# A two-layer block kernel on one Trainium2 core: the first slab after two norms runs on x before the norm's root is known

## The reference

```python
# end of layer 0
hx = hx + g2 * swiglu(fx, ffn_w1[0], ffn_w3[0], ffn_w2[0])
# layer 1: convolution mixer, then feed-forward
ax = modulate(rms_norm(hx, norm_mix[1]), sh1, sc1)      # x*rstd*gain*(1+scale) + shift
yx = conv_mixer(ax, conv_w_in[0], conv_w[0], conv_w_out[0])
hx = hx + g1 * yx
fx = modulate(rms_norm(hx, norm_ffn[1]), sh2, sc2)
hx = hx + g2 * swiglu(fx, ffn_w1[1], ffn_w3[1], ffn_w2[1])   # (silu(f @ w1) * (f @ w3)) @ w2
```

## Time and profile before

| | |
|---|---|
| time, median of 3 runs | 2349.04 us (2348.41 to 2349.38) |
| the profiled execution's own time | 2346.38 us |
| its span in the profile | 2344.7 us |
| TensorE busy | 2243.8 us, 96% |
| VectorE busy | 1129.1 us, 48% |
| ScalarE busy | 729.9 us, 31% |
| GpSimd busy | 29.4 us, 1% |
| mean granted TensorE clock | 0.979 |

### The profile page before, as it was taken

How to read it: one execution, slowest core, us unless ns; L and a number is a source line. 1 busy time by engine, 2 the same in 40 slices (tenths; PEclk the granted TensorE clock), 3 DMA queues, 4 the chain that set the end, 5 groups by cost and what they waited for, 6 DMA issues and landing times.

```text
span 2344.7 us, 25372 instructions
## 1 busy us (share of the span) xinstructions
PE 2243.8 (96%) x9752; PEld 1748.0 (75%) x9752; DVE 1129.1 (48%) x1420; ACT 729.9 (31%) x951; POOL 29.4 (1%) x60
## 2 busy tenths in 40 slices
PE   6999999999899999989989999999999988999996
PEld 4868677686588888868868888887758876878875
DVE  7645343544577333253653323347868647422424
ACT  3221121212343122131233312234555534323321
POOL 0000000000000000000000000000000000000000
PEclk7999999999999999999999999999899999999998
DMA  7232322323187322222212222223201111222220
GB/s 313 72 121 89 121 72 76 120 86 117 61 298 272 108 90 89 92 74 104 90 72 90 100 98 90 89 90 106 72 1 37 37 36 59 102 90 90 90 105 39
DMA packets 32748, 231.88 MB, mean 99 GB/s; under 512 B 3760, under 2 KB 4016, under 8 KB 5552
## 3 DMA queue, kind: packets, MB, share of 16 engines
q1 hardware_dynamic: 23904, 171.98, 20.8%
q0 software_dynamic: 6912, 50.33, 5.7%
q10 hardware_dynamic: 1872, 8.73, 1.0%
HBM read 228.93 MB, written 2.10 MB: 99 GB/s over the span
## 4 chain that ended last, share of the span: by engine, by line
PE 90%; DVE 6%; ACT 2%; issue 1%; DMA 1%; DVEq 0%; POOL 0%; ACTq 0%; POOLq 0%
PE PS L470 26%; PE PS L471 26%; PE PS L472 26%; PE PS L593 4%; PE PS L584 2%; DVE rv L1614 1%; PE PS L848 1%; PE PS L942 1%; PE PS L813 1%; PE PS L932 1%; DVE cv L1967 1%; DMA ada_raw<-ada 1%; DVE w_lo L1511 1%; PE PS L503 0%; PE PS L779 0%
## 5 line engine op out<-in xcount | busy, mean ns | idle before, releaser
L1511 DVE TENSOR_TENSOR w_lo<-raw,w_hi 128x2048 fp32r<-128x2048 f32 x162 | 371.0, 2290 | 670.6 <-ACT w_hi L1072 670.5
L470 PE MATMUL PS<-act_hi,w_hi 128*128 128x512 f32 x1632 | 654.7, 401 | 34.6 <-DVE act_lo L1524 23.4
L1072 ACT ACTIVATE w_hi<-raw 128x2048 fp32r<-128x2048 f32 x162 | 310.1, 1915 | 1105.9 <-PE PS L472 1095.7
L471 PE MATMUL PS<-act_lo,w_hi 128*128 128x512 f32 x1632 | 648.9, 398 | 0.0
L472 PE MATMUL PS<-act_hi,w_lo 128*128 128x512 f32 x1632 | 648.5, 397 | 0.0
L470 PEld LDWEIGHTS PS<-act_hi,w_hi 128*128 128x128 f32 x1632 | 308.8, 189 | 116.6 <-issue 36.9
L471 PEld LDWEIGHTS PS<-act_lo,w_hi 128*128 128x128 f32 x1632 | 308.8, 189 | 76.2 <-issue 1.9
L472 PEld LDWEIGHTS PS<-act_hi,w_lo 128*128 128x128 f32 x1632 | 308.6, 189 | 75.8
L470 PE MATMUL PS<-hid_hi,w_hi 128*128 128x512 f32 (+1 forms) x672 | 266.1, 396 | 0.9 <-ACT sg L1472 0.9
L472 PE MATMUL PS<-hid_hi,w_lo 128*128 128x512 f32 (+1 forms) x672 | 265.4, 395 | 0.0
L471 PE MATMUL PS<-hid_lo,w_hi 128*128 128x512 f32 (+1 forms) x672 | 265.4, 395 | 0.0
(11 more groups left out here) (358 smaller groups left out, 2197.5 us busy)
## 6 DMA issues: line engine op xcount, KB each, us to landing
raw<-slabs SPq DMA_DIRECT2D x162, 1024.0 KB, 4.8
ada_raw<-ada POOLq DMA_DIRECT2D x44, 1024.0 KB, 5.1
early_raw<-ada POOLq DMA_DIRECT2D x4, 1024.0 KB, 21.2
toep<-decay ACTq DMA_DIRECT2D x5, 768.0 KB, 4.2
x<-x_t ACTq DMA_DIRECT2D x1, 2048.0 KB, 9.6
out_t<-x SPq DMA_DIRECT2D x4, 512.0 KB, 2.6
rs<-ctx_t ACTq DMA_DIRECT2D x1, 1024.0 KB, 14.1
con<-consts ACTq DMA_DIRECT2D x1, 642.0 KB, 4.0
```

The costliest lines, as they stand in the source:

```text
L470: pe.matmul(o, w[0], a[0], start=first, stop=False)
L471: pe.matmul(o, w[0], a[1], start=False, stop=False)
L1072: act.activation(w_hi[:, n % 2, :], raw[:, n % 2, :], ACT.Copy).then_inc(w_hi_done, 1)
L1511: dve.tensor_tensor(w_lo[:, k % 2, :], raw[:, k % 2, :], w_hi[:, k % 2, :].bitcast(F32), ALU.subtract).then_inc(w_lo_done, 1)
```

## The change

It does the same to both boundaries.

- Before the norm's root is known, ACT makes `xg_hi` = round(x*gain) and DVE `xg_lo` = x*gain - `xg_hi` for each x tile, right after the tile is added. Two further columns, 512 and 513, hold the shift.
- The first slab (`first_pair`) is multiplied with these. The 512 tokens are cut in two halves of 256, the second with the two shift columns (258), each in a bank of its own: a product is 2 x 3 matmuls instead of 3. The sum of squares stands between input tiles 5 and 6 of this slab, in bank 6.
- The second slab is multiplied with `act_hi`, `act_lo` as before, and these are made as before, after the root.
- When `act_lo` is complete, DVE multiplies the first slab's four banks by `rstd` into `sg` and copies the shift column to `shift_sum`; ACT adds it as a bias (with Silu at boundary 2). Only then come the rest of slab n+2 and the product with the second slab.
- At boundary 1 the squares 1 to 5 are added by GpSimd instead of DVE.
- The last slab of the convolution takes its two output tiles one after the other, no longer interleaved.
- The gain of each norm is computed earlier, and the first pair is taken out of the loop of `up`.

In the diff below, GpSimd comes first, then `first_pair` of TensorE, `first_pair` of ScalarE, `scaled_rest` and `first_pair` of VectorE, and ScalarE's order at boundary 1.

```diff
+            q = nth("mix1")
+            for k in range(1, 6):
+                pool.wait_ge(sq_ready, 8 * q + k + 1)
+                pool.wait_ge(sq_used, 8 * q + k - 1)
+                pool.tensor_tensor(std[:, :], std[:, :], sq[:, k % 2, :], ALU.add).then_inc(sq_used, 1)
...
+            def first_pair(n, name, order, banks, freed):
+                parts, after_x = 8 * nth_split(name + "_x"), 8 * nth_split(name)
+                pe.wait_ge(w_lo_done, n + 1)
+                pe.wait_ge(banks, freed[0])
+                for s, k in enumerate(order):
+                    pe.wait_ge(lo_ready, parts + s + 1)
+                    for m in range(2):
+                        w = wcols(n, k * 256 + m * P, k * 256 + (m + 1) * P)
+                        for half in range(2):
+                            at = slice(half * H, (half + 1) * H + 2 * half)
+                            mm = product(PS[:, BANK_X[name][m][half], 0:H + 2 * half], w, (xg_hi[:, k, at], xg_lo[:, k, at]),
+                                         s == 0, s == KT - 1)
+                    if s == KT // 2:
+                        pe.wait_ge(banks, freed[2])
+                        gathered_sum(nth(name), 6)
+                mm.then_inc(slab_done, 1)
+                pe.wait_ge(w_lo_done, n + 2)
+                pe.wait_ge(banks, freed[1])
+                tile_pair(n + 1, BANK_X[name][2], act, lo_ready, after_x).then_inc(slab_done, 1)
...
+            def first_pair(n, seen, step, func=ACT.Silu):
+                after_static(n)
+                for m in range(2):
+                    act.wait_ge(x_scaled, step + m + 1)
+                    act.activation(sg[:, m, :], sg[:, m, :], ACT.Identity if func == ACT.Copy else func,
+                                   bias=shift_sum[:, m:m + 1]).then_inc(act_silu, 1)
+                after_static(n + 1)
...
+            def scaled_rest(name, s, k):
...
+                dve.scalar_tensor_tensor(out=xg_lo[:, k, 0:T], in0=x[:, k, :], scalar=gain[:, g, k:k + 1],
+                                         in1=xg_hi[:, k, 0:T].bitcast(F32), op0=ALU.mult, op1=ALU.subtract).then_inc(lo_ready, 1)
...
+            def first_pair(n, seen, name, conv=False):
+                b = BANK_X[name]
+                dve.wait_ge(slab_done, n + 1)
+                dve.wait_ge(act_silu, seen + 2)
+                for m in range(2):
+                    dve.tensor_copy(shift_sum[:, m:m + 1], PS[:, b[m][1], H:H + 1])
+                    dve.tensor_tensor(sg[:, m, 0:H], PS[:, b[m][0], 0:H], rstd[:, 0:H], ALU.mult)
+                    dve.tensor_tensor(sg[:, m, H:T], PS[:, b[m][1], 0:H], rstd[:, H:T], ALU.mult).then_inc(x_scaled, 1)
+                static_rest(n + 2)
+                dve.wait_ge(slab_done, n + 2)
...
             if has("conv"):
-                norm("mix1", mod_at(1, 0), CONV - 1, FIN, down_added, 8)
+                for s, k in enumerate(FIN):
+                    act.wait_ge(down_added, KT + s + 1)
+                    scaled("mix1", s, k)
+                    if s == KT - 1:
+                        after_static(CONV - 1)
+                    square(nth("mix1"), s, x[:, k, :])
```

More of the change, by code:

```diff
@@ L372, in build @@
         gathered = ("mix1", "ffn1", "post2", "last")
-        split = [q for q in norms if q not in ("final", "post2", "last")]
+        split = ["mix0", "ctx", "ffn0", "mix1_x", "mix1", "ffn1_x", "ffn1", "pre2", "ffn2"]
         def nth(name):
@@ L676, in down, with swiglu @@
                     gathered_sum(nth(norm))
-            def swiglu(n, seen, added, parts, norm):
+            def swiglu(n, seen, added, parts, done=0):
                 for c, tiles in enumerate(FCH):
@@ L681, in swiglu @@
                         pe.wait_ge(down_added, added + 5)
-                    up(n, tiles, seen, parts)
+                    up(n, tiles, seen, parts, 0 if c else done)
                     n += tiles
@@ L700, in two_turns, with finish_two_turns @@
                         mm.then_inc(slab_done, 1)
-            def finish_two_turns(n, moving, ready, before, free, norm):
+            def finish_two_turns(n, moving, ready, before, free):
                 for j in range(4):
@@ L706, in finish_two_turns @@
                     pe.wait_ge(free, 2 * j + 2)
[L707 to L709 removed]
+                    if j < 3:
+                        tile_pair(n + j, 2 * (j % 2), moving, ready, before).then_inc(slab_done, 1)
+                    else:
+                        out_tile(n + j, 0, bank(2), moving).then_inc(tile_summed, 1)
+                        out_tile(n + j, 1, bank(3), moving).then_inc(slab_done, 1)
             parts_of = lambda name: 8 * nth_split(name)
@@ L1175, in after_static, with scaled, up @@
                     round_slab(n + 2)
-            def up(n, tiles, seen, func=ACT.Silu):
-                with act.Fori(0, tiles // 2) as i:
+            def scaled(name, s, k):
+                g = 3 if name == "mix1" else 4
+                if s == 0:
+                    act.wait_ge(gain_done, g + 2)
+                    at = mod_at(1, 0 if name == "mix1" else 3)
+                    act.activation(xg_hi[:, :, T:T + 2], mod[:, at:at + KT].unsqueeze(2).to_broadcast([P, KT, 2]), ACT.Copy)
+                act.activation(xg_hi[:, k, 0:T], x[:, k, :], ACT.Copy, scale=gain[:, g, k:k + 1]).then_inc(hi_ready, 1)
+            def first_pair(n, seen, step, func=ACT.Silu):
[5 more added lines that the diff above has]
+                after_static(n + 1)
+                for m in range(0 if func == ACT.Copy else 2):
+                    act.wait_ge(hraw_ready, seen + m + 3)
+                    act.activation(hid_hi[:, m, :], hraw[:, m, :], ACT.Copy).then_inc(hid_hi_done, 1)
+            def up(n, tiles, seen, func=ACT.Silu, done=0):
+                with act.Fori(done, tiles // 2) as i:
                     after(n, i)
@@ L1197, in down, with swiglu @@
                     after_static(n + 2 * full - 2 + j)
-            def swiglu(n, seen):
+            def swiglu(n, seen, done=0):
                 for c, tiles in enumerate(FCH):
-                    up(n, tiles, seen)
+                    up(n, tiles, seen, ACT.Silu, 0 if c else done)
                     n += tiles
@@ L1728, in up @@
+            def up(n, tiles, seen, unit0=None, conv=False, done=0):
+                with dve.Fori(done, tiles // 2) as i:
                     if unit0 is not None:
@@ L1789, in norm @@
                 dve.wait_ge(gain_done, gi + 2)
+            def norm(name, gi, layer, shift):
                 at = mod_at(layer, shift)
```

114 lines of the change are left out of this document (81 added, 33 removed).

## The result

The changed kernel takes **2310.88 us** (2310.07 to 2314.42, four runs) against 2348.72 (2347.16 to 2349.38) for the kernel before in the same session: a ratio of 0.984, 95% interval 0.983 to 0.986. The profiled run took 2311.26 us, its span 2309.6.

A forecast was written before the change was run, and what follows sets the result against it. TensorE, busy 96% of the span, was taken as the bound. Boundary gains of 5.7 and 4.9 us made 10.6, giving 2335.8 against the profiled 2346.38 and 2338.5 us for the median; the range went to 2344, main case 2336.5 to 2340.

The forecast's parts named there:

- the sum: Sum of squares on TensorE after five input tiles of the first slab: six passes of 0.429 us plus 0.16 tail.
- Half-width matmuls: First slab at each boundary: matmuls 0.118 us apart, so 11.33 us a slab instead of 11.2.
- x times gain in time: Boundary 1: xg_lo of tile 0 ready at about 997.5, TensorE comes at 1001.75 and never waits.
- Root to second slab: After the sum: act_lo of tile 0 unchanged at 6.65 us behind it; slab n+2 can start 19.9 us behind it.
- The first wait: TensorE finishes slab n and waits 2.56 us for act_lo of tile 0.
- The second: TensorE's wait for w_lo before slab n+2: 0.4 or 2.4 us, depending on the clock.
- The squares at boundary 1: GpSimd's adds taken as 1.3 us each, bounds 0.8 to 1.8; last square ready 0.8 us before the sum.
- A: Rival: GpSimd and VectorE exclude each other at boundary 1, step 2.0 us, sum 1.9 late; 2340.4 to 2342.9 us; 22%.
- B: Rival: clock falls in the second wait, costing 1.7 us at each boundary; time 2341.9 us; 13%.
- C: Rival: GpSimd's first add is slow at boundary 1, last square 3.3 us behind TensorE; time 2341.8 us; 5%.
- D: Rival: a half-width matmul on xg costs as much as a full one, losing 8.5 us per boundary; 2355 us; 3%.
- E: Rival: first slab covers nothing, as xg_lo, a bank or the sum comes late; 2346 to 2350 us; 6%.

The follow-up runs named there:

- kernel at distance 0: Unused tile making weights-to-moving-tiles distance a multiple of 256 bytes: 192 bytes in the changed kernel, 2295.09 us; 224 bytes in the kernel before, 2301.38 us.
- five kernels at distance 64: Changed kernel 2310.88 us; with adds on VectorE 2310.59, adds on 8 numbers 2310.18; kernel before with 8-byte tile behind eps 2319.78, also ahead of weights 2319.07.

## Why the prediction was wrong, point by point

**The step that failed** is in its sum: "5.7 + 4.9 = 10.6 us. Against the profiled execution's own 2346.38 us". It took every stage outside the two boundaries as unchanged, because no instruction of theirs changes. But the diff has a declaration ahead of `std` and `act_hi`, and that changed nearly every full-width matmul. This is shown, not argued: the declaration alone wins 28 us, undoing its shift takes 28.8 us back (2339.70 against 2310.88), and adding more of it gives 2333 or 2295, as the measured pitches say. The diff's other new tiles stand behind the activations or in free space and move none of the old ones.

**What the prediction priced, it priced nearly right**: 10.6 us against 8.3, with the layout held (4.8 and 4.0 us at the boundaries). The missing 0.9 us at each is nearly all one term, *the sum*. It was sized as six passes of 0.429 and a tail of 0.16, 2.74 us. In the kernel with its layout undone it takes from 1010.44 to 1013.96, 3.52 us, 0.8 more than sized: the earlier trace rows are a train of many matmuls, while here each pair of passes starts 1.17 to 1.25 us behind the last, where two passes of 0.429 would fill 0.86. The earlier trace rows held the hint: its L503 row of two passes is 1.10 long, with the sum's end read from it, yet I took the pace from rows 6. The stall is not the squares', since it is the same at boundary 2, where they are long done.

*Half-width matmuls*: 7.14 to 7.19 us for 60, forecast 7.08. *x times gain in time*: yes. *Root to second slab*: 19.92 us behind the sum, forecast 19.9. *The first wait*: 2.29 us, forecast 2.56. *The second*: 1.71 and 1.67, between the 0.4 and 2.4 given for the two clocks, since TensorE took slab n+1 at the pace of `act_lo` (1.45 us a tile). *The squares at boundary 1*: the add takes 1.57 us, inside 0.8 to 1.8, and the last square ends 0.6 us behind the sum's start instead of 0.8 ahead of it; only the sum's third pair of passes needs it, at 1000.14.

**The rivals.** *A*: half right. `xg_lo` grew from 0.75 to 1.13 us beside GpSimd's adds and the step from 1.32 to 1.71, not to 2.0, and none of it reached TensorE: with the adds cut short or given to VectorE the boundary takes 30.64 and 30.65 us, against 30.63. The Trainium skill, SBUF — State Buffer, Who interferes with whom, calls the shared port pair an exclusive lock. In this case's trace the add at 1.57 and an `xg_lo` at 1.13 us overlap, and each of these `xg_lo` pays only 0.38 us: contention, but not one operation behind the other. *B*: the clock stayed at 2.4 GHz behind both waits of the changed kernel; in the experiments it fell behind four of the other first waits, and each time the second wait, 0.40 to 0.76 us long instead of about 1.7, took it up. *C*, *D*, *E*: no sign of them; the half-width pitch on `xg` was 0.1198.

The same section of the Trainium skill (its table of ports) gives TensorE one read port for moving rows and one for weight loads and calls them independent. The pitches between 0.2267 and 0.2376 us, with every other engine idle, say that these two reads are not free of each other.

## What to carry to other kernels

A declaration is part of the machine's work: when a diff adds, drops or resizes a tile, write down the addresses of weights and moving tiles before and after, and compare the pitch of matmuls in a stage that the diff leaves alone before anything is credited to the change. For fp32r matmuls with a weight load each, give weight and moving buffers starts that are multiples of 32 and agree modulo 256 bytes; one unused tile made it worth 47 us here (2348.66 to 2301.38), over five times what the scheduling won. The four executions of each kernel at distance 0 spread by 1.0 and 2.7 us, those of the five kernels at distance 64 by 2 to 11. Where totals spread like that, read a small change from its own stretch of the trace. And read the pace of a short burst from rows of a burst of the same length.

## What the runs showed that was not expected

- The pitch of a full-width fp32r matmul went from 0.2267 to 0.2376 us with nothing but addresses changed: lowest at distance 0 modulo 256 (with starts at multiples of 32), 0.229 or, for whole stages of some executions, 0.2333 at 64, 0.2333 at most other multiples of 32, highest with rows 4 bytes off. The weight load's own duration did not change (0.187 to 0.190 us).
- A GpSimd add of two 128x512 tiles takes 1.57 us beside VectorE, and one of 8 columns 0.51 to 0.68.
- Of twelve waits of TensorE of 2.26 to 2.33 us, eight left its clock at 2.4 GHz and four were followed by a granted clock of 0.64 to 0.68; their lengths don't separate the two.
